# Moving 24 row products from the expert choices of layer 0 into the last groups of its expert loop, with the exponential two tiles later and the first score tiles loaded ahead of a small store

## The reference

```python
mx = jnp.split((cond_x @ mod_w[i] + mod_b[i])[:, None, :], 6, axis=-1)
mc = jnp.split(cond_c @ mod_w[i] + mod_b[i], 6, axis=-1)
hx = x * (1.0 + mx[1]) + mx[0]
hc = ctx * (1.0 + mc[1]) + mc[0]
# PEER, per chunk of tokens h:
q = (h @ wq).reshape(t, PEER_HEADS, 2, PEER_DQ // 2)
s = jnp.einsum('thpd,hpnd->thpn', q, sub_keys)
sv, si = lax.top_k(s, PEER_TOPK)                      # 16 best of 128 keys, twice per head
cand_s = (sv[:, :, 0, :, None] + sv[:, :, 1, None, :])
best_s, best = lax.top_k(cand_s, PEER_TOPK)           # 16 experts per head and token
gate = jax.nn.softmax(best_s, axis=-1)
act = jax.nn.gelu(jnp.einsum('td,thkd->thk', h, u[idx]))
return jnp.einsum('thk,thkd->td', (gate * act), v[idx])
```

## Time and profile before

| | us |
|---|---|
| median of 3 runs (3091.79 to 3094.99) | 3094.75 |
| profiled execution, its own time | 3087.03 |
| profiled execution, span | 3085.2 |
| PE busy in the span | 2770.1 (90%) |
| DVE busy | 2234.7 (72%) |
| ACT busy | 1155.3 (37%) |
| POOL busy | 701.5 (23%) |
| DMA, mean over the span | 203 GB/s |

### The profile page before, as it was taken

One profiled execution on the slowest core, in us unless ns is written; L12 is line 12 of the kernel. 1 busy time (PEld: TensorE's weight loads), 2 busy tenths in 40 slices (PEclk: granted clock), 3 DMA queues, 4 the chain that ended last, 5 costly groups with the idle time before them and its releaser, 6 DMA issues.

```text
span 3085.2 us, 42850 instructions
## 1 busy us (share of the span) xinstructions
PE 2770.1 (90%) x15146; PEld 2388.4 (77%) x15146; DVE 2234.7 (72%) x3885; ACT 1155.3 (37%) x1907; POOL 701.5 (23%) x433
## 2 busy tenths in 40 slices
PE   7999968787787999999999999598898899999997
PEld 3787853577776899999999999464797689999996
DVE  2788868699996877878777877644688656665656
ACT  2333310232374333333333333132447344444443
POOL 0000000233353344443333333000574000000000
PEclk9999979898898999999999999899899999999999
DMA  6322225513378998888888887311266765655563
GB/s 242 110 90 100 83 108 215 181 46 118 122 206 278 334 342 306 309 311 298 286 299 294 283 303 260 117 55 68 91 199 190 255 213 204 216 210 210 205 215 139
DMA packets 237207, 625.77 MB, mean 203 GB/s; under 512 B 17884, under 2 KB 112452, under 8 KB 233412
## 3 DMA queue, kind: packets, MB, share of 16 engines
q1 hardware_dynamic: 200260, 490.52, 45.6%
q0 software_dynamic: 36864, 134.23, 12.6%
HBM read 573.78 MB, written 50.91 MB: 202 GB/s over the span
## 4 chain that ended last, share of the span: by engine, by line
PE 74%; DVE 16%; DMA 4%; ACT 2%; issue 2%; POOL 2%; DVEq 0%; SPq 0%; POOLq 0%; ACTq 0%
PE bank L1007 26%; PE bank L1052 26%; PE bank L826 5%; PE bank L1042 3%; PE bank L880 2%; POOL arena L2042 2%; DVE arena L1816 2%; PE bank L972 2%; DMA arena<-in_wm 2%; PE bank L839 1%; DVE arena L1523 1%; PE bank L799 1%; PE bank L1088 1%; PE bank L933 1%; PE bank L1142 1%
## 5 line engine op out<-in xcount | busy, mean ns | idle before, releaser
L1007 PE MATMUL bank<-h_parts,u_hi 128*128 128x384 f32 (+1 forms) x3712 | 815.9, 310 | 20.1 <-POOL u_lo L2035 12.8
L1052 PE MATMUL bank<-v_parts,p_hi 128*128 128x512 f32 x2560 | 801.9, 395 | 30.1 <-DVE p_lo L1842 29.5
L1007 PEld LDWEIGHTS bank<-h_parts,u_hi 128*128 128x128 f32 x3712 | 637.8, 191 | 37.8 <-issue 13.3
L1007 PE MATMUL bank<-h_parts,u_lo 128*128 128x384 f32 (+1 forms) x1856 | 576.1, 310 | 0.0
L1052 PEld LDWEIGHTS bank<-v_parts,p_hi 128*128 128x128 f32 x2560 | 475.1, 190 | 127.1 <-issue 19.1
L1052 PE MATMUL bank<-v_parts,p_lo 128*128 128x512 f32 x1280 | 503.3, 393 | 0.0
L1838 DVE TENSOR_TENSOR arena<-arena 128x384 f32<-128x384 f32 (+1 forms) x256 | 190.5, 744 | 340.9 <-ACT arena L1387 304.2
L1387 ACT ACTIVATE arena<-bank 128x384 f32<-128x384 f32 (+1 forms) x208 | 90.8, 436 | 719.1 <-PE bank L1007 719.1
L1840 DVE TENSOR_TENSOR v_parts<-arena,v_parts 128x1024 fp32r<-128x1024 f32 x256 | 313.5, 1225 | 63.7 <-ACT v_parts L1390 58.2
L1007 PEld LDWEIGHTS bank<-h_parts,u_lo 128*128 128x128 f32 x1856 | 354.1, 191 | 0.0
L1821 DVE TENSOR_TENSOR u_lo<-arena,u_hi 128x1024 fp32r<-128x1024 f32 x208 | 254.2, 1222 | 81.2 <-ACT u_hi L1302 78.2
(11 more groups left out here) (260 smaller groups left out, 3856.6 us busy)
## 6 DMA issues: line engine op xcount, KB each, us to landing
arena<-in_u SPq DMA_DIRECT2D x256, 512.0 KB, 4.6
arena<-in_v SPq DMA_DIRECT2D x256, 512.0 KB, 3.7
arena<-in_wm SPq DMA_DIRECT2D x80, 512.0 KB, 3.9
arena<-in_wst SPq DMA_DIRECT2D x19, 2048.0 KB, 8.3
gate_scratch<-arena SPq DMA_DIRECT2D x18, 2048.0 KB, 8.7
arena<-gate_scratch SPq DMA_DIRECT2D x32, 768.0 KB, 6.6
arena<-in_whd SPq DMA_DIRECT2D x8, 2560.0 KB, 9.2
arena<-gate_scratch SPq DMA_DIRECT2D x32, 512.0 KB, 4.3
```

Of the source, the lines that this page charges most:

```text
L1007: last = mm(banks[q][:, 0:ND[p]], w[:, q, col], h[:, k, DS[p]], start=(n3 == 0), stop=(n3 == 3 * KT - 1))
L1052: last = mm(banks[2 + 2 * b + half][:, :], x[:, q, b * P:(b + 1) * P], y[:, q, col], start=(first and i == 0), stop=(final and i == 2))
```

## The change

The 24 products of blocks 48 to 63 leave the choices. All 32 late blocks are laid out in a new order, four to a group: one block of chunk 0 (two products), one of chunk 5, and two of chunks 3 and 4 (one product each), so that a group of the loop has four loads and five products instead of two and two. SP issues them at r = 1, 3, 5 and 7; DVE computes them behind the adds of r = 2 (two products), 4, 6 and 8, and adds them to `modcol` with three small additions instead of one. The last four blocks come in the written-out tail, with products after tiles 121 (two), 122, 124 and 126, loaded ahead of tiles 122, 123, 125 and 127. `cb_e` now holds both condition rows, one more 512 KB load. ACT's wait for the products goes. Row chunk 2 is transposed, copied and stored in layer 0, chunk 5 in layer 1 with one PE transpose and one ACT copy there. SP stores the row after the 24 scoring tiles instead of ahead of their first loads. In layer 0 the exponentials stand behind tile 10, in layer 1 still behind tile 8.

```diff
-EXP_AFTER = 8
+EXP_AFTER = [10, 8]
...
-                if p == 0:
-                    for i in range(M_QUERY + 2, M_LOOP):
-                        mod_block(i, wm_q)
                 tile(names, 3)
-                if p == 0:
-                    sp.wait_ge(modT_a, 2)
-                    for x, chunk in enumerate((2, 5)):
-                        rows = modd[1, (CHUNKS + chunk) * D:(CHUNKS + chunk + 1) * D].rearrange("(x d) -> x d", d=P)
-                        sp.dma_start(rows, modT1[:, x, :]).then_inc(mod1_out, 16)
                 sp.wait_ge(qw_l, 16 * (p + 1))
...
                 act_store(K0 - 1)
+                sp.wait_ge(modT_a, 2 + p)
+                at = (CHUNKS + [2, 5][p]) * D
+                sp.dma_start(modd[1, at:at + D].rearrange("(x d) -> x d", d=P), modT1).then_inc(mod1_out, 16)
...
-                        if mods and r in (2, 5):
-                            mod_block(2 * n + (M_LOOP - 16 + r // 4), wm_e)
+                        if mods and r % 2:
+                            mod_block(4 * n + (M_LOOP - 32 + r // 2), wm_e)
...
-                    if p == 0 and j >= NK - 2:
-                        mod_block(M_ALL - NK + j, wm_e)
+                    if p == 0 and j in TAIL_M:
+                        mod_block(M_ALL - 4 + TAIL_M.index(j), wm_e)
...
-            sp.wait_ge(y_pe, 8)
-            for s in range(2):
-                sp.dma_start(cb_q[:, s, :], cs[s, :].partition_broadcast(P)).then_inc(cb_in, 16)
-            for i in range(M_QUERY, M_QUERY + 2):
-                mod_block(i, wm_q)
...
-                if p == 0:
-                    pe.wait_ge(mod_c, 3)
-                    pe.wait_ge(pq_sb, 16)
-                    for x, chunk in enumerate((2, 5)):
-                        last = nc.tensor.transpose(banks[6][0:8, x * P:(x + 1) * P], modcol[:, 1, 16 * chunk + 1:16 * chunk + 16:2], ident)
-                    last.then_inc(mod_t, 1)
+                pe.wait_ge(mod_c, 3 + p)
+                pe.wait_ge(pq_sb, 16 * (p + 1))
+                at = 16 * [2, 5][p]
+                nc.tensor.transpose(banks[6][0:8, 0:P], modcol[:, 1, at + 1:at + 16:2], ident).then_inc(mod_t, 1)
...
-                        if p == 0 and i == 0 and n == 2:
-                            act.wait_ge(wm_b, 2 + M_LOOP)
...
-                if p == 0:
-                    act.wait_ge(mod_t, FIRST + 2)
-                    af_(modT1.rearrange("p c d -> p (c d)"), banks[6][0:8, 0:2 * P], ACT.Copy).then_inc(modT_a, 1)
+                act.wait_ge(mod_t, FIRST + 2 + p)
+                af_(modT1, banks[6][0:8, 0:P], ACT.Copy).then_inc(modT_a, 1)
...
-                    dve.wait_ge(cb_in, 64)
-                    for k in range(KT):
-                        mod_pair(M_QUERY + k, cb_q, wm_q, spare_q, k)
-                    for k in range(KT):
-                        mod_one(M_QUERY + 8 + k, cb_q[:, 1, :], wm_q, mod_col(5 * KT + k), mod_col(5 * KT + k))
...
-                        if r in (3, 6):
-                            x = r // 6
+                        if r % 2 == 0:
+                            x = r // 2 - 1
+                            dve.wait_ge(wm_in[x % 2], 32 * n + (16 * (M_LOOP // 2) - 256 + 16 * (x // 2) + 16))
+                            block = wm_e[:, x % 2, :]
                             if x == 0:
-                                dve.wait_ge(wm_c, n - 7)
-                            dve.wait_ge(wm_in[x], 16 * n + (16 * (M_LOOP // 2) - 128 + 16))
-                            block = wm_e[:, x, :]
-                            V.tensor_tensor_reduce(block, block, cb_e, 1.0, 0.0, ALU.mult, ALU.add, few[:, x:x + 1]).then_inc(wm_b, 1)
+                                dve.wait_ge(wm_c, 3 * n - 23)
+                                V.tensor_tensor_reduce(spare_e, block, cb_e[:, 0, :], 1.0, 0.0, ALU.mult, ALU.add, few[:, 0:1]).then_inc(wm_a, 1)
+                                dve.wait_ge(wm_a, n + (M_NORM - 8 + 1))
+                            V.tensor_tensor_reduce(block, block, cb_e[:, 1, :], 1.0, 0.0, ALU.mult, ALU.add, few[:, x + 1:x + 2]).then_inc(wm_b, 1)
...
-                        if j >= NK - 2:
-                            n = 4 * KT + KT - NK + j
-                            mod_one(M_ALL - NK + j, cb_e, wm_e, mod_col(n), mod_col(n))
+                        if j == TAIL_M[0] - 1:
+                            mod_pair(M_ALL - 4, cb_e, wm_e, spare_e, KT - 1)
+                        elif j + 1 in TAIL_M:
+                            x = TAIL_M.index(j + 1)
+                            n = [0, 6 * KT - 1, 5 * KT - 2, 5 * KT - 1][x]
+                            mod_one(M_ALL - 4 + x, cb_e[:, 1, :], wm_e, mod_col(n), mod_col(n))
```

More of the change, by code:

```diff
@@ L317, in build @@
         afbf = ar(B_M + 1024, 1024, c=2, n=512)
-        modT1 = arena[0:8, B_T + 1024:B_T + 1024 + 2 * P].rearrange("p (c d) -> p c d", c=2)
+        modT1 = arena[0:8, B_T + 1024:B_T + 1024 + P]
         ijw = ar(B_C, 3 * ND_MAX, c=3, t=ND_MAX)
@@ L394, in build @@
         BLOCKS_M = 4
+        TAIL_M = [122, 123, 125, 127]
         sums = small[:, 113:113 + 2 * BLOCKS_M]
-        few = small[:, 113:115]
-        M_WOUT, M_NORM, M_QUERY, M_LOOP, M_ALL = 32, 40, 48, 64, 80
+        few = small[:, 113:118]
+        M_WOUT, M_NORM, M_LOOP, M_ALL = 32, 40, 48, 80
         spare = ar(A_KC + 768, D)
-        cb_q, wm_q, spare_q = ar(A_OT, 2 * D, s=2, d=D), ar(A_OT + 2 * D, 2 * D, s=2, d=D), ar(A_LN + 8192, D)
-        cb_e, wm_e = ar(A_HD, D), ar(A_LN + 4096, 2 * D, s=2, d=D)
+        cb_e, wm_e, spare_e = ar(A_HD, 2 * D, s=2, d=D), ar(A_LN + 4096, 2 * D, s=2, d=D), ar(A_LN + 6144, D)
         modT = arena[0:32, A_KC + 512:A_KC + 512 + 2 * P].rearrange("p (s d) -> p s d", s=2)
@@ L701, in ln_row @@
                         sp.dma_start(ln_b, a["ln_b"][p, 1].partition_broadcast(P)).then_inc(ln_in, 16)
-                    elif i == 4:
-                        sp.dma_start(cb_e, cs[1, :].partition_broadcast(P)).then_inc(cb_in, 16)
+                    elif i < 6:
+                        sp.dma_start(cb_e[:, i - 4, :], cs[i - 4, :].partition_broadcast(P)).then_inc(cb_in, 16)
                 def experts_and_row(j, q, N):
@@ L710, in peer @@
                     sp.wait_ge(tok_done, 1)
-                    sp.wait_ge(mod1_out, 32)
+                    sp.wait_ge(mod1_out, 16)
                     group(nB, experts_and_row)
@@ L717, in peer @@
                 else:
+                    sp.wait_ge(mod1_out, 32)
                     ln_rows(p, 1, STREAMS[p], LN_BASE[p], [], x_of)
@@ L748, in _ @@
             ln_rows(0, 0, [0, 1], 0, range(4), x_of)
-            for i in range(M_WOUT + 2, M_QUERY):
+            for i in range(M_WOUT + 2, M_LOOP):
                 mod_block(i, wm)
             peer_first(0)
-            sp.wait_ge(y_pe, 8)
-            for s in range(2):
-                sp.dma_start(cb_q[:, s, :], cs[s, :].partition_broadcast(P)).then_inc(cb_in, 16)
-            for i in range(M_QUERY, M_QUERY + 2):
-                mod_block(i, wm_q)
             peer(0)
@@ L1021, in peer @@
                         pe.wait_ge(pq_sb, 16 * (p + 1))
-                        if p == 0:
-                            pe.wait_ge(modT_a, 2)
+                        pe.wait_ge(modT_a, 2 + p)
                     if n >= 2:
@@ L1337, in peer @@
                     ahead(j)
-                    if j == EXP_AFTER:
+                    if j == EXP_AFTER[p]:
                         gate_exponentials()
@@ L1517, in mod_pair @@
                 dve.wait_ge(wm_b, i + 2)
-                pair = M_WOUT + (i - M_WOUT if i < M_QUERY else i - M_QUERY + 8)
                 for s in range(2):
                     if s:
-                        dve.wait_ge(wm_a, pair + 1)
+                        dve.wait_ge(wm_a, (i if i < M_NORM else 47) + 1)
                     col = modcol[:, 1, 2 * n + s:2 * n + s + 1]
@@ L1900, in peer @@
                         V.tensor_copy(s_tok[:, bass.ds(20 * n - 32, 20)], s20).then_inc(dots, 1)
-                    dve.wait_ge(cb_in, 80)
+                    dve.wait_ge(cb_in, 64)
                     dve.wait_ge(g_out[1], 1 + 16 * SPILLS[0][1])
@@ L1930, in peer @@
                     dve.wait_ge(wm_b, 2 + M_ALL)
+                    dve.wait_ge(wm_c, 1 + 3 * 7)
                     m = modcol[:, 1, 8 * KT:10 * KT]
@@ L2117 @@
     wm = [x["mod_w"][l].T.reshape(CHUNKS, KT, P, D) for l in range(DEPTH)]
-    wm = np.concatenate([wm[0][2:].reshape(-1, P, D)] + [wm[1][c] for c in (1, 2, 0, 5, 3, 4)])
+    late = np.stack([wm[1][0], wm[1][5], wm[1][3:5].reshape(KT, 2, P, D)[:, 0], wm[1][3:5].reshape(KT, 2, P, D)[:, 1]], axis=1)
+    wm = np.concatenate([wm[0][2:].reshape(-1, P, D), wm[1][1], wm[1][2], late.reshape(4 * KT, P, D)])
     keys = x["peer_keys"].transpose(0, 4, 1, 2, 3).reshape(DEPTH, P, 16 * NK)
```

9 lines of the change are left out of this document (6 added, 3 removed).

## The result

| | before | after |
|---|---|---|
| median, us | 3093.27 (4 runs, 3089.99 to 3094.99) | 3062.97 (4 runs, 3056.19 to 3065.41) |
| ratio, 95% interval | | 0.9904 [0.9892, 0.9916] |
| profiled execution, its own time | 3087.03 | 3056.19 |
| profiled execution, span | 3085.2 | 3054.4 |

The change takes 30 us off, where I had forecast 23.7. The direction and the mechanism hold; the size doesn't, and 3062.97 lies 2 us under the range. The forecast of 3071 was carried over from a median of three runs, 3094.75; the table has a fourth.

A forecast was written before the change was run, and what follows sets the result against it. It took PE to bound the expert loop and DVE's products and choices to bound layer 0 before the gates. Terms -22.7 + 0 + 0 - 1.3 + 0.3 = -23.7 us, from 3094.75 to 3071 us; range 3065 to 3080.

The forecast's parts named there:

- 22.7 us earlier. That is the main term.: Layer 0: without the 24 products, DVE's choices start at about 591.75 instead of 614.41, 22.7 us earlier.
- part of it is lost: Rival: set 1 of the scores copied too late or more stalls, 6 to 12 us lost, 3077 to 3083; chance 0.12.
- I keep 14 us: Layer 0 choices: stalls beyond 122.0 us undisturbed stay at 14 us, the same conversions falling at other moments.
- 4 us less: Lower end of the stall range in the choices: conversions come singly where four came together; upper end 6 us more.
- more is won: Rival: stalls in the choices fall to half, 7 us further off, 3064 us; chance 0.05.
- the prediction's walk by it: Estimate of choice stalls by the shared-port rule: 17 us after against 19 today, making the sum 1.4 us lower.
- Exponentials and order of the loads, 0.: Layer 0 scoring: later exponentials and the store moved behind the tiles are worth 0, under 17 us of cover.
- Moved in, the loop, 0.: Expert loop: 16 loads of 512 KB and 24 products added cost 0, with 3 us above allowed.
- Tail, -1.3: Behind tile 127: the last product goes ahead of that tile and off the chain, -1.3 us.
- layer 1, +0.3: Ahead of layer 1's scoring: one added transpose and ACT copy on the chain, +0.3 us (0 to 0.8).
- Covered anyway: Rival: another engine, scoring, would set the end of the choices; 3094 us, no change; chance 0.03.
- slower: Rival: the loop's loads fall a tile behind, `u` late at 14 tiles, +63, 3134 us; chance 0.04.

The follow-up runs named there:

- a_again: The changed kernel as it is, measured and profiled a second time: 3064.97 us, ratio 0.9908 to the kernel before.
- c: Kernel before, products left in place, with ACT's weight parts of units 8 to 11 moved ahead of its wait for the products: 3083.51 us, ratio 0.9969 to before.
- d: Changed kernel plus one ACT wait that forces POOL's four conversions for units 8 to 11 into a row again: 3071.85 us, ratio 0.9929 to before.
- e_old_order: Changed kernel with layer 0's exponential back behind tile 8 and the store back ahead of the first score-tile loads: 3060.91 us, ratio 0.9901 to before.
- k: Changed kernel with layer 0's exponentials ahead of the first score tile, so no tile is converted during the choices: 3088.44 us, ratio 0.9989 to before.
- b_removed: Kernel before without the 24 products and their 16 loads, everything else where it was: 3063.33 us, ratio 0.9907 to before.
- h_loads_doubled: Changed kernel with a second, unread 512 KB load beside each of the loop's 28 modulation blocks: 3062.18 us, ratio 0.9901 to before.
- n: Changed kernel with all 64 layer 0 candidate additions on POOL and the exponentials behind tile 7: 3053.04 us, ratio 0.9872 to before.

## Why the prediction was right or wrong

- **"22.7 us earlier. That is the main term."** Right: 22.95, with the idle time of 29.4 us ahead of the first choice. The later sets kept ahead as worked out (615.16 for 615.6), so that "part of it is lost" didn't come.
- **"I keep 14 us" of stalls in the choices.** This is the step that failed, together with the end of its range, "4 us less". The forecast took the same 20 conversions at other moments to cost the same. Counted as it did, against 122.0 us without stalls, they cost 14.3 before and 9.8 after (11.5 in a_again), although 22 conversions now fall there; the choices fell by 4.5 us (2.8 in a_again). What conversions cost depends on how they stand: additions that meet a row wait for its end. Four in a row, 9.4 us long, held four additions for 6.3 to 6.8 us where they came within 3.3 us of its start, for 4.30 where they came 5.4 behind it (before), and for 2.10 where they came 7.6 behind it (c, whose row ends at 687.16). The products had made such a row, and its additions came early in it. d, which puts it back beside the same 22 conversions, loses 6.9 us by the medians and 5.4 in the choices; c, which takes its four conversions out of the choices, gains 9.6 by the medians. The prediction's reason against the rival "more is won", that the first four tiles' conversions still come in a row, was true (6.54 us at 670.02), but it spoke of the row that stays, and the other one goes: additions busy 26.0 us before, 21.4 and 23.0 after, 12.6 without tiles. That the total lies near this rival's 3064 is luck: its stalls were to fall to half, and they fell by a third.
- The Trainium skill, page SBUF — State Buffer, section "SBUF: two separate sides", lets the GpSimd instruction that started first keep the shared ports, and the prediction's walk by it gave 1.4 us less. The trace agrees with the sign and with who waits; the ends at 676.42 and 676.56 show more than one instruction's length, since VectorE was not let in between two conversions that follow each other. The same holds for the earlier trace rows, which the prediction read as plain agreement.
- **The rest of the miss.** The profiled span fell by 30.8 us instead of 23.7. Of these 7.1 us, 4.5 are the choices and 2.8 the way from the subtraction to tile 25, where 2 were allowed; the other terms give 0.2 back. The remaining 0.9 us between 3071 and 3062.97 comes of carrying one execution over to a median: the profiled one lay 7.7 us under the median that I started from, and lies 6.8 under the one after.
- **Exponentials and order of the loads, 0.** Right, by e_old_order. The cover was there: k shows what it costs when it goes.
- **Moved in, the loop, 0.** Right, by b_removed, and with room, by h_loads_doubled. PE never waits, not at tile 123 either.
- **Tail, -1.3, and layer 1, +0.3.** The product is gone from the chain. Layer 1's copy takes 0.15 us there; loop and tail are 0.98 shorter, the way to layer 1's scoring 0.31 longer.
- **"Covered anyway" and "slower"** fell: no sign of either.
- The 2.8 us from the subtraction to tile 25 I can't place: they are 0.4 in the profile of a_again, so that they are within what one execution differs from another. Their cause stays open.

## What to carry to other kernels

When a piece of work is taken out, follow also what stood in the queue behind its waits: where a wait had gathered instructions of another engine into one burst, that burst goes too; here it was worth an eighth to a fifth of the main term. Small two-input operations of VectorE beside long conversions on GpSimd cost by how the conversions stand; subtracting their busy time from the stage's length shows at once whether they are all of the difference, but read their cost from the stretches between their neighbours, not from a sum that counts overlaps twice. Where both engines want the same moments, try giving the small ones to the engine with the long instructions: here all 64 there won some 10 us, 48 of them some 4, which is not told from none.

## What the runs showed of the hardware

- Four additions of 128x16 to 128x48 take 0.50 us on VectorE alone, and up to 6.76 beside a row of four GpSimd conversions of 2.4 us each; they end with the last of the row (676.42 and 676.56). Where they met a single conversion they took 0.6 to 2.7 us. MAX8, FIND_INDEX8 and MATCH_REPLACE8 are not held up (at most 0.30, 0.30 and 0.28 us in all profiles).
- GpSimd does the same four additions in 0.84 to 0.86 us (n), beside conversions of 128x1024 in 2.4.
- Loads of 512 KB and more at 341 GB/s over 400 us, DMA engines busy 0.92, left TensorE without a gap at a granted clock of 1.00.
